# One gate matmul fewer per recurrence step, and diagonal copies on another engine

## The reference

```
h = rms_norm(x);  one projection h @ w_in is cut into parts
A: indexer scores -> top-k keys per query -> softmax attention over them (6 heads, 2 kv heads)
B: HGRN2 gated linear recurrence (6 heads, key and value 128 wide), chunk by chunk
C: cross attention into 256 memory tokens (4 heads)
merged = sum over A, B, C of  sigmoid(gate_b) * (y_b @ w_out_b)        # gates = 3 x 1024 columns of h @ w_in
x = x + rms_norm(merged @ w_out);   x = x + rms_norm(relu(rms_norm(x) @ w_up)^2 @ w_down)
```

## Time and profile before

| | us |
|---|---|
| median of 3 runs | 2380.3 |
| the profiled execution | 2379.09 |
| span of its trace, first to last instruction | 2377.3 |
| TensorE busy | 2276.0 (96%) |
| VectorE busy | 1225.2 (52%) |
| ScalarE busy | 699.2 (29%) |
| GpSimd busy | 640.9 (27%) |

### The profile page before, as it was taken

One profiled execution on the slowest core, in us unless ns is written; L12 is line 12 of the kernel. 1 busy time (PEld: TensorE's weight loads), 2 busy tenths in 40 slices (PEclk: granted clock), 3 DMA queues, 4 the chain that ended last, 5 costly groups with the idle time before them and its releaser, 6 DMA issues. The chain is left out here.

```text
span 2377.3 us, 40572 instructions
## 1 busy us (share of the span) xinstructions
PE 2276.0 (96%) x16446; PEld 2120.2 (89%) x16446; DVE 1225.2 (52%) x2134; ACT 699.2 (29%) x1428; POOL 640.9 (27%) x724
## 2 busy tenths in 40 slices
PE   6989999999999999889998998979999999999997
PEld 6989999999999888778888998969889899898896
DVE  4125699999990777155533544163333233233335
ACT  5224412222211233455544323242112122121121
POOL 3453531112311787100001211151121212121213
PEclk9999999999999999999999999979999999999999
DMA  5342222232223643532226433140201102012014
GB/s 167 110 117 76 65 85 93 88 97 87 95 89 124 185 135 103 160 98 73 62 62 217 148 112 111 36 141 20 71 18 53 53 19 69 19 51 71 18 55 157
DMA packets 210564, 214.54 MB, mean 90 GB/s; under 512 B 33776, under 2 KB 191792, under 8 KB 210416
## 3 DMA queue, kind: packets, MB, share of 16 engines
q1 hardware_dynamic: 210416, 212.49, 28.7%
HBM read 153.03 MB, written 59.43 MB: 89 GB/s over the span
## 5 line engine op out<-in xcount | busy, mean ns | idle before, releaser
L264 POOL TENSOR_TENSOR w_lo<-w_raw,w_hi 128x2048 fp32r<-128x2048 f32 (+2 forms) x41 | 173.9, 4243 | 631.0 <-ACT w_hi L257 631.0
L2512 POOL TENSOR_TENSOR w_lo<-w_raw,w_hi 128x2048 fp32r<-128x2048 f32 x31 | 143.0, 4614 | 580.5 <-ACT w_hi L2536 580.5
L277 PE MATMUL ps<-f_hi,w_hi 128*128 128x384 f32 (+1 forms) x768 | 252.1, 328 | 1.8 <-DVE ff_relu_sq L2573 1.8
L277 PE MATMUL ps<-f_hi,w_lo 128*128 128x384 f32 (+1 forms) x768 | 251.2, 327 | 0.0
L277 PE MATMUL ps<-f_lo,w_hi 128*128 128x384 f32 (+1 forms) x768 | 251.2, 327 | 0.0
L277 PE MATMUL ps<-h_hi,w_lo 128*128 128x384 f32 (+1 forms) x768 | 250.5, 326 | 0.0
L277 PE MATMUL ps<-h_lo,w_hi 128*128 128x384 f32 (+1 forms) x768 | 250.4, 326 | 0.0
L277 PE MATMUL ps<-h_hi,w_hi 128*128 128x384 f32 (+1 forms) x768 | 250.3, 326 | 0.0
L662 ACT ACTIVATE b_stage<-ps 128x256 f32<-128x256 f32 (+5 forms) x203 | 83.4, 413 | 514.7 <-PE ps L277 499.0
L2594 DVE TENSOR_TENSOR big<-big,ps 128x512 f32<-128x512 f32 x144 | 94.8, 658 | 262.5 <-PE ps L277 244.5
L2581 DVE TENSOR_TENSOR ff_relu_sq<-ff_relu_sq 128x384 f32<-128x384 f32 (+1 forms) x96 | 101.2, 1054 | 223.9 <-ACT ff_relu_sq L2545 223.6
(11 more groups left out here) (231 smaller groups left out, 5407.7 us busy)
## 6 DMA issues: line engine op xcount, KB each, us to landing
w_raw<-in_w_in SPq DMA_DIRECT2D x34, 1024.0 KB, 5.6
w_raw<-in_w_up SPq DMA_DIRECT2D x16, 1024.0 KB, 5.5
w_raw<-in_w_down SPq DMA_DIRECT2D x16, 1024.0 KB, 5.3
gm_gate<-d_gate SPq DMA_DIRECT2D x48, 192.0 KB, 2.5
d_gate<-gatef_stage SPq DMA_DIRECT2D x28, 192.0 KB, 3.4
gm_y_raw<-d_y SPq DMA_DIRECT2D x8, 576.0 KB, 5.1
n_x<-in_x_prompt SPq DMA_DIRECT2D x8, 512.0 KB, 7.3
w_raw<-in_w_mem_kv SPq DMA_DIRECT2D x4, 1024.0 KB, 7.2
```

What stands on the lines that cost most here:

```text
L264: engine.tensor_tensor(g.w_lo[:, s, 0:size], g.w_raw[:, s, 0:size], g.w_hi[:, s, 0:size].bitcast(F32), ALU.subtract).then_inc(g.w_split, 1)
L277: last = pe.matmul(out, left(a, kk), right(b, kk), start=(kk == 0 and n == 0), stop=(kk == k - 1 and n == 2))
L2512: G.tensor_tensor(g.w_lo[:, slot, :], g.w_raw[:, slot, :], g.w_hi[:, slot, :].bitcast(F32), ALU.subtract).then_inc(g.w_split, 1)
```

## The change

`PER_TICK` goes from 6 to 5 and `LEAD_IN_A` from 24 to 72. The counts become 48 + 5 x 90 = 498 up to the end of the recurrence, 72 + 42 = 114 at the attention's beginning, 290 in the slots and 106 behind the last. The diagonal copies leave VectorE: ScalarE does them one tick behind the fifth near level, and VectorE waits for them only before it writes the same half of `sdiag` again.

```diff
-LEAD_IN, PER_TICK = 48, 6
+LEAD_IN, PER_TICK = 48, 5
...
             fl.round_next(act, 0)
+            def keep_diagonal(i):
+                pos = levels(i).index(NEAR[-1])
+                act.wait_ge(lv_free, lv_of[i, pos])
+                for k0 in range(0, rows(i), DIAG):
+                    last = S.activation(smat[k0:k0 + DIAG, i % 2, :, k0:k0 + DIAG], sdiag[k0:k0 + DIAG, i % 2], ACT.Copy)
+                last.then_inc(d_done, 1)
+
             for tick in range(N_TICK):
+                for i in at([t + 2 * len(NEAR) - 1 for t in FIRST_TICK], tick):
+                    keep_diagonal(i)
...
                 if i >= 2 and pos == 0:
                     dve.wait_ge(qk_done, qk_of[i - 2, "q"])
+                    dve.wait_ge(d_done, i - 1)
...
-                if s == NEAR[-1]:
-                    dve.wait_ge(lv_free, lv_of[i, pos])
-                    for k0 in range(0, t, DIAG):
-                        last = V.tensor_copy(smat[k0:k0 + DIAG, i % 2, :, k0:k0 + DIAG], held[k0:k0 + DIAG])
-                    last.then_inc(d_done, 1)
...
-LEAD_IN_A, PER_TURN, PER_SLOT = 24, 3, (2, 3)
+LEAD_IN_A, PER_TURN, PER_SLOT = 72, 3, (2, 3)
```

## The result

| | before | after |
|---|---|---|
| median of 16 runs each | 2379.8 | 2391.6 |
| lowest and highest | 2374.2, 2384.5 | 2379.6, 2395.2 |
| the profiled execution, its span | 2379.1, 2377.3 | 2385.3, 2383.1 |

The ratio is 1.0045, with a 95% interval from 1.0034 to 1.0056: some 11 us slower, where I forecast 2381.7 and at most 2390. The profiled execution lost only 6.2 us. So there are two questions: what this execution lost, and what a usual one loses besides.

The account below looks back on a forecast made before the run. TensorE was taken to bound the kernel, busy 96% of the span, with GpSimd and VectorE close behind in the recurrence. Terms -14.0 + 8.5 + 6.9 = +1.4 us gave 2381.7 us, range 2374 to 2390.

Parts of the forecast that it names:

- The 58 slots keep their five matmuls.: Attention slots: each slot's count of gate matmuls stays the same, so no time was charged there.
- the attention's beginning: Recurrence's end to first score matmul: 48 more gate matmuls don't fit the idle time, since a late store stalls; +8.5 us.
- The recurrence: All 90 ticks: 90 gate matmuls fewer and the diagonal copies off VectorE gain 14.0 us, bounds 9.1 and 16.2.
- The matmuls: Recurrence: 90 gate matmuls less at 0.1645 us each are worth 14.8 us where TensorE is the bound.
- the idle time of the first steps: First nine ticks of the recurrence: TensorE waits for VectorE and GpSimd there, so 1.5 us are not gained.
- GpSimd's pieces: Rest of the recurrence: weight-splitting pieces on GpSimd move and exceed its slack, costing 2.1 us.
- The copies' 2.8 us: Recurrence after the ninth tick: TensorE idle time behind VectorE's diagonal copies goes, gaining 2.8 us, bounds 0 and 2.92.
- GpSimd gains up to 8.7 us: Recurrence: without 34 VectorE copies holding the shared port, GpSimd loses up to 8.7 us of blocking.
- rival 1: Attention's beginning: idle time takes the 48 matmuls, +0.9 us instead of +8.5; total 2374.1 us, chance 0.15.
- Behind the last slot: After the attention's slots: 42 more gate matmuls with no idle time to fill cost 6.9 us, bounds 6.2 and 7.3.
- rival 2: Recurrence: GpSimd and VectorE become its bound, so it gains only 5 us; total 2390.7 us, chance 0.17.
- Rival 3: Recurrence and attention's beginning: copies hid more than their stalls and the store lands early; total 2371.9 us, chance 0.08.

Follow-up runs that it names:

- the second profile: Profile from rerunning the changed kernel without an edit, beside the kernel before; that series measured a median of 2386.5 us, ratio 1.0031.
- the first profile: Profile of the changed kernel's first series, against the kernel before; the profiled execution took 2385.3 us, the median was 2391.6 us, ratio 1.0045.

## Why the prediction was wrong, by its own steps

**The step that failed** is in the part on the last gate matmuls: "The 58 slots keep their five matmuls." I costed the slots at nothing because their count didn't change. What hangs on the count of gate matmuls issued so far did: every eviction in the slots moved 42 / 5 = 8.4 slots later, and one of them brought its rounding in front of copies that the transposes of the last tile wait for. That is 1.09 us of idle time, and with it in most profiles the clock of 1.2 GHz, some 8 us more in the slots. With that rounding elsewhere the change takes 2380.9 us, where I forecast 2381.7. To come so near was partly luck: the terms that I had, as measured below, add up to -11.1 + 7.9 + 6.4 = +3.2 us and not +1.4. I had followed this rule for the attention's beginning, where I counted the units, and not for the slots.

**The recurrence**: -14.0 forecast, -11.1 measured (205.21 us to 194.07 in the second profile, below, both with a clock of 0.93 in the first steps; the first profile's -9.8 contains a lower one, 0.88). Within the bounds, below the term. The matmuls, the idle time of the first steps and GpSimd's pieces were together sized right: 14.8 - 1.5 - 2.1 = 11.2, and without the copies 206.52 to 195.74, 10.8. The copies' 2.8 us was the mis-sized term. At six matmuls per step they are worth 206.52 - 203.47 = 3.05 us of the recurrence, 2.1 of them idle time of TensorE; a second pair, both at 0.93 in the first steps, gives the same (205.21 - 202.33 = 2.88). At five they are worth 195.74 - 195.37 = 0.4, from one pair. With the counts alone TensorE's wait for the state update, which queues behind the copies, is already down from 1.5 to 0.4 us although VectorE still makes them: I added two gains that share idle time. That GpSimd's pieces are what the copies' stall lies inside is my reading; no run takes them apart. The two windows of the second profile of the changed kernel:

```profile
768.93:793.60 24.67, 19.70 (x280) 18.21 (x280) 13.35 (x13) 3.31 (x4) 17.58 (x18) 0.93 0.95 270
793.60:963.00 169.40, 164.12 (x2981) 144.04 (x2982) 119.75 (x219) 74.37 (x252) 130.99 (x153) 0.99 0.42 118
```

By the rule of the Trainium skill (SBUF — State Buffer, "Who interferes with whom"), an exclusive lock that VectorE's copies and GpSimd share, I estimated that GpSimd gains up to 8.7 us with the copies gone from VectorE. The profiles don't show this gain: in the recurrence GpSimd is busy for 17.81 + 131.82 = 149.6 us before, and for 149.6 with ScalarE's copies alone. Its two multiplications of the query take 53.5 + 16.2 us in the kernel before, and then 49.8 + 20.0. The first kind became shorter and the second longer by as much. What agrees with that rule is that none of ScalarE's 34 copies takes over 0.364 us, where VectorE's longest took 1.859. Their groups by line, of before and of the kernel with the copies alone:

```profile
L1429 POOL TENSOR_TENSOR hr_query<-hr_query,hr_tree 128x384 f32<-128x384 f32 x48 | 53.5, 1116 | 19.3 <-PE ps L1302 19.3
...
L1429 POOL TENSOR_TENSOR hr_query<-hr_query,hr_forget 128x768 f32<-128x768 f32 x8 | 16.2, 2026 | 9.2 <-PE ps L1302 9.1
```

```profile
L1438 POOL TENSOR_TENSOR hr_query<-hr_query,hr_tree 128x384 f32<-128x384 f32 x48 | 49.8, 1038 | 16.0 <-PE ps L1302 15.7
...
L1438 POOL TENSOR_TENSOR hr_query<-hr_query,hr_forget 128x768 f32<-128x768 f32 x8 | 20.0, 2504 | 10.3 <-PE ps L1302 10.2
```

**The attention's beginning**: +8.5 forecast, +7.9 measured. The store landed 18.4 us behind the recurrence (20.0), and 14.2 us followed (13.3). The stall stood where it was put, behind the second key transpose, and rival 1 (the idle time takes the 48) was wrong. **Behind the last slot**: +6.9 forecast, +6.4 measured; all that follows took 1.0 us more, where I had nothing, but 3.0 less in the second profile.

**The rivals**: rival 2 gave about the right time, 2390.7, for a wrong reason. The recurrence gained 11 us and not 5. Rival 3 needed a store that lands before 13.3 us; it landed at 18.4.

## What to carry to other kernels

When a count of background work is changed, list everything that is triggered by that count and find its new place, in stages that keep their rate too: what moved here was one ScalarE operation of 1 us. Look then at what queues behind it on its engine, and at whether TensorE stands still there, since the clock behind a short wait can cost several times the wait (here 1.1 us, and some 8 behind it). One execution's profile can miss such a loss when it strikes only in some executions, as the first profile here did; the median and the spread of the runs don't.

## What the runs showed of the hardware

An idle time of 1.09 to 1.28 us among the last tile's narrow matmuls was followed by the lower clock (0.50 for 10 us and more) in 4 of the 5 profiles that have it. None of the nine profiles without it has such a stretch there. In the four the clock rose again only once the gate matmuls behind the last slot ran. In the kernel before a longer wait elsewhere was followed by no such fall (the clock is 1.00 from 1050 to 1070 us):

```profile
1050.43 0.82 PE L1785 MATMUL ps<-at_room,at_val 128*128 128x128 f32 x5 [2.25 <-ACT at_room L1860]
```

Score matmuls of 384 columns stood ahead of that one. What of the narrow matmuls and of the idle time each does to the clock wasn't taken apart.

The Trainium skill (TensorE: Matmul & The Clock Gate, "A second HAM failure mode: psum-queue depth-cycling") says of another kernel that short idle times between groups of matmuls came often enough to make the clock fall and rise again and again. The traces here agree in that the idle time ahead of the fall was short, about 1.1 us, but it was a single one.
